# Expert stage of a two-block transformer kernel: the down product from native fp32 to three split passes

## The chip, the cores and the metric

The kernel runs on one core of a Trainium2 chip as a single program. The metric is the device time of one execution in microseconds (us); lower is better. Three executions of the kernel before took 2968.38, 2960.40 and 2960.74 us, median 2960.74 us.

## What is computed

The reference is a first block (a modulated token mixer and a mixture-of-experts feed-forward layer over 512 tokens of width 1024) and a second block (two attention layers, each with a convolutional feed-forward layer). The change concerns the mixture of experts. Each token goes to 8 of 64 experts, and for every block of at most 128 rows that belong to one expert the reference does:

```python
xb = hpad[rows]
y = (jax.nn.silu(xb @ we_gate[e]) * (xb @ we_up[e])) @ we_down[e]
acc = acc.at[rows].add(y * rw[:, None].astype(y.dtype))
```

`we_gate[e]` and `we_up[e]` are 1024x256, `we_down[e]` is 256x1024, all fp32.

## The kernel before, in words

The program is a row of stages, each a block in which every engine runs its own instructions in order and engines meet through semaphores. `experts` is the longest stage. It handles 66 blocks: 62 written out, one expert each, and the rest in a loop whose length is found at run time.

The work of one block b is spread over the engines:

- **SyncE** (SP queue) loads the expert's weights as three transfers of 1 MB, two of gate and up weights (`load_gu`) and one of down weights (`load_dn`), into `raw` buffers of which every one exists twice. The order of issue is gate-and-up of block b, then down of block b-2. Line 1297 issues all of them.
- **ScalarE** (ACT) writes the high part of each quarter of the gate-and-up weights, rounded to the fp32r type (`high_gu`, L1395), the high part of the turned rows (`high_x`, L1405), SiLU (L1400), and copies PSUM to SBUF: the block's result (`copy_y`, L1413) and the turned activations (`copy_act`, L1418).
- **VectorE** (DVE) writes the low parts, the number less its high part (`low_gu`, L1446; `low_x`, L1453), multiplies gate and up (`activate`, L1459), reads the token numbers of a later block from PSUM (L1469, L1474), aims its store (L1464), and prepares the selection of a block after that (`choose`, L1489).
- **GpSimd** (POOL) issues the indirect gather of rows of block b+2 (L1524) and the indirect store of block b-2 (L1531).
- **TensorE** (PE) runs, in step b: `find(b+2)`, a small product (L1333); `gate_and_up(b)`, 8 pieces of the depth in three passes each (L1351); `turn(b+1)`, 8 transposes (L1340); `down(b-1)` (L1363); and `turn_act(b)`, 2 transposes (L1371).

A product in three passes takes high by high, high by low and low by high, with fp32r operands. `down` alone takes its operands unsplit: the turned activations `act_t` in fp32 and the raw down weights:

```python
for k in range(2):
    mm = pe.matmul(ps[:, BY + n, :], at[:, k * P:(k + 1) * P], ex.chunk(GU + k, s)[:, half],
                   start=(k == 0), stop=(k == 1))
```

The order on each engine is fixed by the function `step` of that engine. On ScalarE step b is: three `high_gu` of b, `silu(b-1)`, `high_x(b)`, the fourth `high_gu` of b, `copy_y(b-2)`, `copy_act(b-1)`. On VectorE it is: three `low_gu` of b, `activate(b-1)`, `low_x(b)`, the fourth `low_gu` of b, `aim(b-2)`, `read_tokens(b+2)`, `choose(b+3)`. On GpSimd it is: `gather(b+2)`, `store(b-2)`.

The attention stages, later in the program, split their weights in the same way, with the high parts on ScalarE and the low parts on GpSimd (L2096).

Of the kernel before, what the change touches and what calls it, by code (L numbers as in the profile page):

```python
# [1241 lines left out]
def experts(m, d, scratch, ex):  # L1242
# [9 lines left out]
    with stack:  # L1252
# [7 lines left out]
        at = sb("act_t", [P, 2 * P])  # L1260
# [3 lines left out]
         a_done, a_turned, at_done, y_made, y_out, target_done, own_s, issued, pool_seen) = (  # L1264
            sem(n) for n in ("picked", "listed_at", "listed", "xt_turned", "xt_high", "xt_low", "gu_high", "gu_low",
                             "gu_used", "sg_done", "a_done", "a_turned", "at_done", "y_made",
# [26 lines left out]
        with nc.Block() as block:  # L1293
            @block.sync
            def _(sp):
# [8 lines left out]
                def load_dn(b, s, e):  # L1304
                    sp.wait_ge(y_made, value(2 * b - 2))
                    load(GU // 2, s, e)
# [19 lines left out]
            def _(pe):  # L1326
# [28 lines left out]
                def down(c, s, h):  # L1355
                    pe.wait_ge(at_done, value(c + 1))
                    pe.wait_ge(ex.arrived(GU + 1, s), value(16 * h + 16))
                    for n in range(2):
                        if some(2 * c + (n - 2)):
                            pe.wait_ge(y_out, value(2 * c + (n - 1)))  # L1360
                        half = slice(n * 512, (n + 1) * 512)
                        for k in range(2):
                            mm = pe.matmul(ps[:, BY + n, :], at[:, k * P:(k + 1) * P], ex.chunk(GU + k, s)[:, half],  # L1363
                                           start=(k == 0), stop=(k == 1))
                        mm.then_inc(y_made, 1)
# [24 lines left out]
            def _(act):  # L1390
# [23 lines left out]

                def copy_act(b):
                    act.wait_ge(a_turned, value(b + 1))
                    act.wait_ge(y_made, value(2 * b))
                    act.activation(at[:], ps[:, BA, 0:2 * P], ACT.Copy).then_inc(at_done, 1)  # L1418

                def step(b, s, h):  # L1420
# [8 lines left out]
                    if some(b - 1):  # L1429
                        copy_act(b - 1)  # L1430

# [5 lines left out]
                copy_act(end - 1)  # L1437
                copy_y(end - 1, 1, half - 1)

            @block.vector  # L1440
            def _(dve):
# [14 lines left out]
                def activate(b):  # L1456
                    dve.wait_ge(sg_done, value(b + 1))
                    dve.wait_ge(a_turned, value(b))
                    dve.scalar_tensor_tensor(a[:], ps[:, BG, D_EXP:], row(found, b, 2), sg[:], ALU.mult, ALU.mult).then_inc(a_done, 1)  # L1459

# [30 lines left out]
                def step(b, s, h):  # L1491
# [8 lines left out]
                    read_tokens(b + 2, s, h + 1)  # L1500
                    choose(b + 3)
# [11 lines left out]
                activate(end - 1)  # L1513
                aim(end - 2, 0, half - 1)
# [3 lines left out]
            def _(pool):  # L1518
# [14 lines left out]

                def step(b, s, h):
                    gather(b + 2, s)
                    if some(b - 2):
# [6 lines left out]
                end, half = Count(pairs, 2, FIRST), Count(pairs, 1, FIRST // 2)  # L1543
                store(end - 2, 0, half - 1)
# [912 lines left out]
```

## Time and profile before

| | |
|---|---|
| median of 3 runs | 2960.74 us |
| the profiled execution | 2961.6 us |
| its span | 2959.8 us |
| granted TensorE clock, mean | 0.927 |
| PE busy | 2577.0 us (87%) |
| DVE busy | 1650.0 us (56%) |
| ACT busy | 1165.8 us (39%) |
| POOL busy | 253.6 us (9%) |
| expert stage, first to last gate-and-up product | 664.2 to 1334.2 us |

The span is the time from the first to the last instruction. Shares are over the whole program; the stage in question has shares of its own. A busy PE is modelled from the starts of its instructions, so neighbouring matmuls overlap in the rows: their spacing is read from their starts.

### The profile page before, as it was taken

Reading aid. Unit: us, or ns where it says so; the run is one execution under the profiler, and the core shown is the slowest. Engines: PE = TensorE matmul, PEld = TensorE weight load, DVE = VectorE, ACT = ScalarE, POOL = GpSimd, SP = SyncE. Lnnn points to the kernel's source line nnn. Section 1 sums busy time; section 2 is a strip of 40 time slices with the busy share of each in tenths; the row PEclk is TensorE's granted clock in tenths of the full one; section 3 lists DMA queues with packets and bytes.
Section 4 is the critical chain, followed back from the end, with each engine's and each line's share of the span. In section 5 each row is a group of like instructions: output and inputs, shape, how many; then the busy total and the mean of one; then the engine's idle time right before and its main releaser. Section 6 shows DMA issues by size and latency. Waiting matters only on the chain. (4 is left out here: it accounts for less than half of the span.)

```text
span 2959.8 us, 30515 instructions
## 1 busy us (share of the span) xinstructions
PE 2577.0 (87%) x10494; PEld 1794.2 (61%) x10494; DVE 1650.0 (56%) x2733; ACT 1165.8 (39%) x1797; POOL 253.6 (9%) x186
## 2 busy tenths in 40 slices
PE   6998998469999999992599988999968884899998
PEld 2443556337776777671366666888746662678886
DVE  2392663437777777776355545636535546366473
ACT  2003432216666666661233334424323323354242
POOL 0000000001111222120122100000012210000000
PEclk9999898589999999996699999999989996899999
DMA  6102121318999999986211013232221101222322
GB/s 275 57 0 83 63 86 57 144 38 322 360 350 357 358 358 348 365 325 244 85 64 43 0 57 112 83 113 90 71 107 43 43 0 43 71 85 92 107 84 73
DMA packets 77263, 418.70 MB, mean 141 GB/s; under 512 B 17312, under 2 KB 17440, under 8 KB 40160
## 3 DMA queue, kind: packets, MB, share of 16 engines
q1 hardware_dynamic: 57856, 383.67, 35.1%
q0 software_dynamic: 19296, 33.60, 3.1%
q8 instruction: 63, 1.03, 0.1%
q14 instruction: 48, 0.39, 0.0%
HBM read 415.10 MB, written 38.80 MB: 153 GB/s over the span
## 5 line engine op out<-in xcount | busy, mean ns | idle before, releaser
L1446 DVE TENSOR_TENSOR w_gu_low<-raw,w_gu_high 128x1024 fp32r<-128x1024 f32 x264 | 322.8, 1223 | 121.7 <-ACT w_gu_high L1395 108.9
L1395 ACT ACTIVATE w_gu_high<-raw 128x1024 fp32r<-128x1024 f32 x264 | 279.8, 1061 | 109.0 <-PE banks L1351 107.8
L2270 PE MATMUL banks<-h_high,w_high 128*128 128x512 f32 x704 | 276.8, 393 | 33.0 <-DVE w_low L2333 33.0
L2270 PE MATMUL banks<-h_low,w_high 128*128 128x512 f32 x704 | 275.6, 391 | 0.0
L2270 PE MATMUL banks<-h_high,w_low 128*128 128x512 f32 x704 | 275.4, 391 | 0.0
L1363 PE MATMUL banks<-raw,act_t 128*128 128x512 f32 x528 | 237.6, 593 | 0.9 <-ACT act_t L1418 0.9
L1351 PE MATMUL banks<-w_gu_high,x_t_high 128*128 128x512 f32 x528 | 213.9, 405 | 2.0 <-DVE x_t_low L1453 2.0
L1351 PE MATMUL banks<-w_gu_high,x_t_low 128*128 128x512 f32 x528 | 207.9, 394 | 0.0
L1351 PE MATMUL banks<-w_gu_low,x_t_high 128*128 128x512 f32 x528 | 207.6, 393 | 0.0
L2333 DVE TENSOR_TENSOR w_low<-raw,w_high 128x2048 fp32r<-128x2048 f32 (+2 forms) x76 | 152.9, 2012 | 87.3 <-ACT w_high L2298 87.2
L2298 ACT ACTIVATE w_high<-raw 128x2048 fp32r<-128x2048 f32 (+2 forms) x76 | 128.0, 1684 | 170.8 <-PE banks L2280 152.7
L2270 PEld LDWEIGHTS banks<-h_high,w_high 128*128 128x128 f32 x704 | 133.3, 189 | 65.6 <-issue 38.0
L1524 POOL DMA_INDIRECT x_rows<-h_rows,token_i x68 | 69.7, 1024 | 1172.8 <-DVE token_i L1474 1164.3
L1363 PEld LDWEIGHTS banks<-raw,act_t 128*128 128x128 f32 x528 | 95.2, 190 | 95.8 <-issue 94.7
L2270 PEld LDWEIGHTS banks<-h_high,w_low 128*128 128x128 f32 x704 | 133.1, 189 | 27.9
L2270 PEld LDWEIGHTS banks<-h_low,w_high 128*128 128x128 f32 x704 | 133.2, 189 | 27.5
L2280 PE MATMUL banks<-hidden_high,w_high 128*128 128x512 f32 x352 | 141.6, 402 | 2.5 <-DVE w_low L2333 2.5
L2310 ACT ACTIVATE conv<-up,vec 128x512 f32<-128x512 f32 x88 | 70.6, 815 | 184.9 <-DVE up L2348 184.9
L2280 PE MATMUL banks<-hidden_high,w_low 128*128 128x512 f32 x352 | 137.1, 390 | 0.0
L2280 PE MATMUL banks<-hidden_low,w_high 128*128 128x512 f32 x352 | 137.0, 389 | 0.0
L1351 PEld LDWEIGHTS banks<-w_gu_high,x_t_low 128*128 128x128 f32 x528 | 99.7, 189 | 22.7
L590 PE MATMUL banks<-h,w_in 128*128 128x512 f32 (+3 forms) x256 | 101.9, 561 | 12.9 <-DMA w_in<-in_w_in 12.9
(356 smaller groups left out, 4865.9 us busy)
## 6 DMA issues: line engine op xcount, KB each, us to landing
raw<-in_w_e SPq DMA_DIRECT2D x198, 1024.0 KB, 9.1
raw<-in_w_up SPq DMA_DIRECT2D x44, 1024.0 KB, 4.8
w_ada<-in_w_ada_later SPq DMA_DIRECT2D x16, 1024.0 KB, 4.8
expert_rows<-y_rows SPq DMA_DIRECT2D x16, 1024.0 KB, 11.3
w_qkv<-in_w_even SPq DMA_DIRECT2D x8, 1536.0 KB, 6.3
raw<-in_w_down SPq DMA_DIRECT2D x16, 768.0 KB, 4.2
w_qkv<-in_w_odd SPq DMA_DIRECT2D x8, 1536.0 KB, 6.3
raw<-in_w_down SPq DMA_DIRECT2D x16, 640.0 KB, 3.9
```

Of the source, the lines that this page charges most:

```text
L590: mm = pe.matmul(bank[0:cols, 0:t[1]], wt(name)[:, k, j * P:j * P + cols], m.h[:, k, t[0]:t[0] + t[1]], start=(k == 0), stop=(k == KT - 1))
L1351: mm = pe.matmul(ps[:, BG, :], xp[:, k, :], wp[:, j, :], start=(k == 0 and i == 0), stop=(k == KT - 1 and i == 2))
L1363: mm = pe.matmul(ps[:, BY + n, :], at[:, k * P:(k + 1) * P], ex.chunk(GU + k, s)[:, half], start=(k == 0), stop=(k == 1))
L1395: act.activation(w_gu[c].high[:].rearrange("p j n -> p (j n)"), ex.chunk(c, s), ACT.Copy).then_inc(gu_high, 1)
L1446: dve.tensor_tensor(w_gu[c].low[:].rearrange("p j n -> p (j n)"), ex.chunk(c, s), w_gu[c].high[:].rearrange("p j n -> p (j n)").bitcast(F3 ...
L1524: pool.indirect_dma_start(xg[s][:], None, scratch["h_rows"], bass.IndirectOffsetOnAxis(ap=token_i[s][:, 0:1], axis=0), bounds_check=SEQ - ...
L2270: mm = pe.matmul(ps[:, 2 * s + c, :], wp[:, at:at + P], hp[:, k, :], start=(k == 0 and i == 0), stop=(k == KT - 1 and i == 2))
L2280: mm = pe.matmul(ps[:, 4 + s, :], wp[:, k * P:(k + 1) * P], hp[:, k, :], start=(k == 0 and i == 0), stop=(k == b - a - 1 and i == 2))
L2298: act.activation(w[s].high[:, 0:cols], raw[s][:, 0:cols], ACT.Copy).then_inc(high_done, 1)
L2310: act.activation(y[s][:, c, :], up[s][:, c, :], ACT.Identity, scale=tap(t, c, 2), bias=tap(t, c, 3)).then_inc(tap0, 1)
L2333: dve.tensor_tensor(w[s].low[:, 0:cols], raw[s][:, 0:cols], w[s].high[:, 0:cols].bitcast(F32), ALU.subtract).then_inc(low_done, 1)
```

## The change

The down product takes the same three passes as gate and up. The activations get a high part, written by ScalarE in `copy_act`, and a low part, written by VectorE in a new `low_act`. The down weights get a high part, written by ScalarE in a new `high_dn` as four instructions of 128x512, and a low part, written by GpSimd in a new `low_dn`, also four. There is one buffer `w_dn` for each part. The raw buffer of the down weights is free for its next load once `low_dn` has read it, and no longer once the product is made.

```diff
-        at = sb("act_t", [P, 2 * P])
+        at, w_dn = Split(sb, "act_t", [P, 2 * P]), Split(sb, "w_dn", [P, 2, D])
...
                 def load_dn(b, s, e):
-                    sp.wait_ge(y_made, value(2 * b - 2))
+                    sp.wait_ge(dn_low, value(4 * b - 4))
...
                 def down(c, s, h):
                     pe.wait_ge(at_done, value(c + 1))
-                    pe.wait_ge(ex.arrived(GU + 1, s), value(16 * h + 16))
...
                         for k in range(2):
-                            mm = pe.matmul(ps[:, BY + n, :], at[:, k * P:(k + 1) * P], ex.chunk(GU + k, s)[:, half],
-                                           start=(k == 0), stop=(k == 1))
+                            pe.wait_ge(dn_low, value(4 * c + (2 * n + k + 1)))
+                            for i, (ap, wp) in enumerate(at.passes(w_dn)):
+                                mm = pe.matmul(ps[:, BY + n, :], ap[:, k * P:(k + 1) * P], wp[:, k, half],
+                                               start=(k == 0 and i == 0), stop=(k == 1 and i == 2))
                         mm.then_inc(y_made, 1)
...
+                def high_dn(c, s, h):
+                    act.wait_ge(ex.arrived(GU, s), value(16 * h + 16))
+                    for n in range(2):
+                        if some(2 * c + (n - 2)):
+                            act.wait_ge(y_made, value(2 * c + (n - 1)))
+                        for k in range(2):
+                            act.activation(w_dn.high[:, k, n * 512:(n + 1) * 512], ex.chunk(GU + k, s)[:, n * 512:(n + 1) * 512],
+                                           ACT.Copy).then_inc(dn_high, 1)
...
-                    act.activation(at[:], ps[:, BA, 0:2 * P], ACT.Copy).then_inc(at_done, 1)
+                    act.activation(at.high[:], ps[:, BA, 0:2 * P], ACT.Copy).then_inc(at_high, 1)
...
                     if some(b - 1):
                         copy_act(b - 1)
+                        high_dn(b - 1, *later(s, h, -1))
...
+                def low_act(b):
+                    dve.wait_ge(at_high, value(b + 1))
+                    dve.tensor_tensor(at.low[:], ps[:, BA, 0:2 * P], at.high[:].bitcast(F32), ALU.subtract).then_inc(at_done, 1)
...
                     read_tokens(b + 2, s, h + 1)
+                    if some(b - 1):
+                        low_act(b - 1)
                     choose(b + 3)
...
+                def low_dn(c, s):
+                    for n in range(2):
+                        for k in range(2):
+                            half = slice(n * 512, (n + 1) * 512)
+                            pool.wait_ge(dn_high, value(4 * c + (2 * n + k + 1)))
+                            pool.tensor_tensor(w_dn.low[:, k, half], ex.chunk(GU + k, s)[:, half],
+                                               w_dn.high[:, k, half].bitcast(F32), ALU.subtract).then_inc(dn_low, 1)
...
                 def step(b, s, h):
                     gather(b + 2, s)
+                    if some(b - 1):
+                        low_dn(b - 1, (s + 1) % 2)
                     if some(b - 2):
                         store(b - 2, *later(s, h, -2))
```

The order of ScalarE's instructions over one step in the middle of the expert stage, in the changed kernel (`raw_0_11` and `raw_1_11` are the two copies of the raw buffers; line numbers are the changed kernel's):

```order
L1414 ACTIVATE y_block_15<-banks 128x512 x2
L1428 ACTIVATE act_t_high<-banks 128x256
L1422 ACTIVATE w_dn_high<-raw_0_11 128x512 x4
L1396 ACTIVATE w_gu_high<-raw_0_11 128x1024 x3
L1401 ACTIVATE silu_gate<-banks 128x256
L1406 ACTIVATE x_t_high<-banks 128x512 x2
L1396 ACTIVATE w_gu_high<-raw_0_11 128x1024
```

The four new copies stand between the copy of the activations and the first three quarters of the next block's gate-and-up weights. Nothing else has changed its place.

The order on GpSimd over one step, before:

```order
L1524 DMA x_rows_15<-h_rows,token_i_15 128x1024
L1531 DMA y_rows<-y_block_15,target_i_15 4096x1024
```

and in the changed kernel:

```order
L1543 DMA x_rows_15<-h_rows,token_i_15 128x1024
L1558 TENSOR_TENSOR w_dn_low<-raw_0_11,w_dn_high 128x512 x4
L1550 DMA y_rows<-y_block_15,target_i_15 4096x1024
```

The four subtractions stand behind a gather and ahead of a store.

## Rows read from the trace of the kernel before

**Rows 1.** One stretch of the expert stage: columns are us, busy us of each engine (instructions), granted PE clock, DMA share, GB/s

```profile
1000.00:1100.00 100.00, 100.00 (x451) 70.48 (x450) 71.62 (x108) 68.64 (x97) 21.04 (x20) 1.00 0.98 359
```

**Rows 2.** Timeline of TensorE over one block: start, us, operation

```profile
1002.32 0.48 PE L1351 MATMUL banks<-w_gu_high,x_t_high 128*128 128x512 f32 x1
...
1007.22 0.39 PE L1351 MATMUL banks<-w_gu_high,x_t_high 128*128 128x512 f32 x1
1007.45 0.39 PE L1351 MATMUL banks<-w_gu_low,x_t_high 128*128 128x512 f32 x1
...
1008.78 3.60 PE L1363 MATMUL banks<-raw,act_t 128*128 128x512 f32 x8
1012.22 0.38 PE L1371 MATMUL banks<-const,act 128*128 128x128 f32 x2
...
1012.54 0.48 PE L1351 MATMUL banks<-w_gu_high,x_t_high 128*128 128x512 f32 x1
```

**Rows 3.** Timeline of DVE, ACT and POOL in that block, with idle time before

```profile
1002.69 0.38 ACT L1418 ACTIVATE act_t<-banks 128x256 f32<-128x256 f32 x1
...
1003.73 1.02 POOL L1524 DMA_INDIRECT x_rows<-h_rows,token_i  x1 [7.91 <-DVE token_i L1474]
...
1004.05 1.06 ACT L1395 ACTIVATE w_gu_high<-raw 128x1024 fp32r<-128x1024 f32 x1 [0.97 <-PE banks L1351]
...
1005.05 1.00 POOL L1531 DMA_INDIRECT y_rows<-y_block,target_i  x1 [0.31 <-issue]
1005.14 1.23 DVE L1446 TENSOR_TENSOR w_gu_low<-raw,w_gu_high 128x1024 fp32r<-128x1024 f32 x1 [1.68 <-ACT w_gu_high L1395]
...
1007.89 1.23 DVE L1446 TENSOR_TENSOR w_gu_low<-raw,w_gu_high 128x1024 fp32r<-128x1024 f32 x1
...
1008.55 1.08 ACT L1405 ACTIVATE x_t_high<-banks 128x512 fp32r<-128x512 f32 x2
...
1010.62 1.22 DVE L1446 TENSOR_TENSOR w_gu_low<-raw,w_gu_high 128x1024 fp32r<-128x1024 f32 x1
```

**Rows 4.** DVE's groups by line from 1000 to 1300 us: busy, mean ns, idle before

```profile
L1446 DVE TENSOR_TENSOR w_gu_low<-raw,w_gu_high 128x1024 fp32r<-128x1024 f32 x117 | 143.1, 1223 | 53.7 <-ACT w_gu_high L1395 48.5
L1453 DVE TENSOR_TENSOR x_t_low<-banks,x_t_high 128x512 fp32r<-128x512 f32 x59 | 37.8, 681 | 0.0
L1489 DVE TENSOR_TENSOR pick<-const,dest 128x512 bf16<-128x512 f32 x26 | 17.7, 682 | 0.0
L1459 DVE SCALAR_TENSOR_TENSOR act<-banks,found,silu_gate 128x256 f32<-128x256 f32 x29 | 13.9, 478 | 0.0
```

**Rows 5.** One line of ScalarE in the attention stages: min/median/max ns

```profile
L1745 ACT ACTIVATE h_high<-o x16: 612/613/629, 1715.2 to 2506.0; 128x512 fp32r<-128x512 f32 x16
```

**Rows 6.** Timeline of POOL and DVE at the start of the first attention stage

```profile
1444.79 2.35 POOL L2096 TENSOR_TENSOR w_v_low<-w_qkv,w_v_high 128x1024 fp32r<-128x1024 f32 x1
...
1446.42 1.88 DVE L2081 TENSOR_TENSOR rope<-rope,rstd 128x512 f32<-128x512 f32 x2 [14.47 <-DMA amask<-in_amask]
...
1451.44 2.79 DVE L2016 TENSOR_TENSOR crossed<-banks,rope 32x512 f32<-32x512 f32 x4
1451.85 2.34 POOL L2096 TENSOR_TENSOR w_q_low<-w_qkv,w_q_high 128x1024 fp32r<-128x1024 f32 x1 [4.71 <-ACT w_q_high L1979]
```

**Rows 7.** Those two lines of DVE in both attention stages: min/median/max ns

```profile
L2081 DVE TENSOR_TENSOR rope<-rope,rstd x4: 678/964/1276, 1446.4 to 2182.6; 128x512 f32<-128x512 f32 x4
...
L2016 DVE TENSOR_TENSOR crossed<-banks,rope x128: 679/686/695, 1451.4 to 2429.1; 32x512 f32<-32x512 f32 x128
```

**Rows 8.** DMA from 1000 to 1100 us: totals

```profile
DMA packets 6994, 35.87 MB, mean 359 GB/s; under 512 B 2072, under 2 KB 2072, under 8 KB 3169
```

**Rows 9.** A stretch in which the input projection's weights are loaded, columns as rows 1

```profile
60.00:74.00 14.00, 9.31 (x17) 4.13 (x18) 0.45 (x1) 0.22 (x1) 0.00 (x0) 0.69 0.98 414
```

**Rows 10.** SP's issue of down weights at 1012.41 us, and its time to landing

```profile
1012.41 0.33 SPq L1297 DMA_DIRECT2D raw<-in_w_e  x1
...
raw<-in_w_e SPq DMA_DIRECT2D x1, 1024.0 KB, 13.2
```

More of the change, by code:

```diff
@@ L1263, in experts @@
         (picked, listed_at, listed, xt_turned, xt_high, xt_low, gu_high, gu_low, gu_used, sg_done,
-         a_done, a_turned, at_done, y_made, y_out, target_done, own_s, issued, pool_seen) = (
+         a_done, a_turned, at_high, at_done, dn_high, dn_low, y_made, y_out, target_done, own_s, issued, pool_seen) = (
             sem(n) for n in ("picked", "listed_at", "listed", "xt_turned", "xt_high", "xt_low", "gu_high", "gu_low",
-                             "gu_used", "sg_done", "a_done", "a_turned", "at_done", "y_made",
+                             "gu_used", "sg_done", "a_done", "a_turned", "at_high", "at_done", "dn_high", "dn_low", "y_made",
                              "y_out", "target_done", "own", "issued", "pool_seen"))
@@ L1437, in _ @@
                 copy_act(end - 1)
+                high_dn(end - 1, 1, half - 1)
                 copy_y(end - 1, 1, half - 1)
@@ L1513, in _ @@
                 activate(end - 1)
+                low_act(end - 1)
                 aim(end - 2, 0, half - 1)
@@ L1543, in _ @@
                 end, half = Count(pairs, 2, FIRST), Count(pairs, 1, FIRST // 2)
+                low_dn(end - 1, 1)
                 store(end - 2, 0, half - 1)
```

## The prediction

> **What bounds the kernel now.** I read the stretches of the expert stage first, then the timeline of one block, then the groups by line. In the stretches PE is busy for 100.00 of 100 us at a granted clock of 1.00, while DVE and ACT are busy for 71.62 and 68.64 us and POOL for 21.04 [rows 1]. In the timeline one block's first gate-and-up pass starts at 1002.32 and the next one's at 1012.54 [rows 2], so a block takes 10.22 us, and nothing stands idle on PE between. So the stage is bound by PE's own work, but the next limits are near: the DMA engines have a share of 0.98 [rows 1].
>
> **What the change removes.** The down product is eight PE instructions that start at 1008.78 and are followed by the next operation at 1012.22 [rows 2]: 3.44 us, 0.43 each. Passes with fp32r operands of the same 128x512 shape start 0.23 us apart [rows 2]. The change makes twelve of them, 12 x 0.228 = 2.74 us. PE is relieved of 0.70 us a block, and PE alone would need 9.52 us. Over 66 blocks that would be 46 us.
>
> **What it adds, engine by engine.**
>
> ACT: four copies SBUF to SBUF of 128x512. The same form takes 613 ns [rows 5]. Back to back a copy starts about 0.1 us before the one ahead has ended: the two of x_t_high take 1.08 us together [rows 3], where the pair would be 1.19 apart from that. So the four cost 4 x 0.52 = 2.1 us. ACT's load goes from 0.6864 x 10.22 = 7.0 us to 9.1 us, which still fits into 9.52 with hardly a gap.
>
> DVE: `low_act`, 128x256 with one input in PSUM. Nearest is activate, 478 ns for 128x256 [rows 4]; I take 0.45. DVE's load goes from 7.3 to 7.8 us.
>
> POOL: four subtractions of 128x512. The trace has them at twice the size, 2.35 us [rows 6]. Half of that, 1.17 us, is the lower bound, 1.3 with some fixed part the upper. I take 1.17, since the row is almost all slope if DVE's pair (1223 for 1024, 682 for 512 elements [rows 4]) is a guide: its fixed part is 0.14 us. That is 4.7 us a block, and POOL goes from 2.1 to 6.8. Taken alone it fits.
>
> SP: `load_dn` waits for `low_dn` instead of for the product. `low_dn` of a block is done before its product, so this wait is over sooner, and the loads ahead of it in the queue still set the time of issue: nothing gained or lost.
>
> **The price that decides: two engines at one port.** Loads add up only if the engines don't hinder each other, and the attention stages show that they do. A POOL subtraction runs from 1444.79 to 1447.14. DVE starts the first of two multiplications with both inputs in SBUF at 1446.42 [rows 6]. The shortest of its line takes 678 ns; the longest took 1276 [rows 7], and since the pair takes 1.88 us [rows 6] this one is it: it ended at 1447.70, 0.55 us after POOL, so it did all but its first 0.13 us once POOL was through. But `crossed`, with one input in PSUM, takes 2.79 us for four beside a POOL subtraction [rows 6], and 679 to 695 ns in all 128 cases [rows 7]. So a DVE operation whose inputs both lie in SBUF stands still while a POOL subtraction runs. This agrees with the Trainium skill (SBUF — State Buffer, Who interferes with whom): such a DVE instruction contends with a GpSimd instruction that reads SBUF, and the second to be issued blocks fully. No row here shows POOL as the second.
>
> In the expert stage five of DVE's operations a block are of that kind: four of w_gu_low (1223 ns) and one of pick (682) [rows 4]. Those of x_t_low and activate read PSUM and are free.
>
> I lay one block out, from the start of its gate-and-up product (1002.32 is zero). ACT ends the copy of act_t at 0.75 [rows 3], the four new copies at 2.9, and the first three w_gu_high at 3.9, 4.9 and 5.9; the first ended at 2.8 before [rows 3]. POOL's gather starts at 1.4 and with its 0.3 us behind is over at 2.7 [rows 3]. Then POOL and DVE take turns:
>
> - POOL's first subtraction 2.7 to 3.9; first w_gu_low 3.9 to 5.1
> - second subtraction 5.0 to 6.2; second w_gu_low 6.1 to 7.3
> - third subtraction 7.2 to 8.4; third w_gu_low 8.3 to 9.5
> - fourth subtraction 9.4 to 10.6, beside activate and x_t_low, which end at 11.1; fourth w_gu_low 11.1 to 12.3
>
> The third w_gu_low ended at 6.8 before [rows 3]. The next gate-and-up product needs x_t_low at 11.1. The down product needs the fourth subtraction at 10.6, then 0.7 us for its last three passes and 0.3 for what follows: 11.6. So a block takes 11.1 to 11.6 us; the fourth w_gu_low now ends after the next product has begun, where it used to end 0.7 us ahead, which moves the gather and with it POOL. DVE's own sum says the same: 7.8 of work and three POOL operations in front of its w_gu_low, 3 x 1.05 = 3.15, is 10.9, and some of its old idle 1.68 us ahead of the first w_gu_low [rows 3] stays. I take 11.4.
>
> **The sum.** 64 blocks x (11.40 - 10.22) = +75.5 us. At the end the last block's weights are split with nothing beside: 0.6 + 4 x 1.17 + 0.7 = 6.0 us in place of 3.44, +2.5. The profiled execution took 2961.6 us; with +78 it would be 3039.6. That execution was 0.9 us above the median, so 3039. For 10.9 to 11.9 us a block the same sum gives 3006 to 3070, the forecast's own range. PE then idles about 1.9 us a block in short pieces; I price no loss of clock for this, since the granted clock was 1.00 in the stretch.
>
> **Rivals.**
>
> *No exclusion here, and the DMA sets the pace: faster.* The turning point is plain: if a POOL subtraction holds DVE for so little that DVE's waits stay under 10.2 - 7.8 = 2.4 us a block in all, and they don't lie on the way to x_t_low, the block gets shorter. It can't reach 9.52. A block moves 3.67 MB (35.87 MB in 100 us [rows 8]). At the rate of this stage brought to full share, 359 / 0.98 = 366 GB/s, that needs 10.0 us. Loads alone went faster elsewhere, 414 GB/s at 0.98 [rows 9], so with luck it is 9.52, PE's own. At 10.0 the gain is 0.22 x 64 = 14, less 2.5 at the end: 2949; at 9.52, 2918. For it: PE is the only bound today. Against it: [rows 6, 7]. Chance 0.17, of which 0.05 for under 2942.
>
> *No change.* The exclusion is weak, and the down weights come late. They must be there when ACT has copied act_t, 0.75 us into the next block, and no longer only at the down product. Those issued at 1012.41 took 13.2 us, to 1025.6 [rows 10], while ACT would want them at 1022.76 + 0.75 = 1023.5. ACT would stand 2 us with the next w_gu_high behind it, in those blocks in which the DMA queue is long. Then 10.2 us a block remain: 2961. The Trainium skill (DMA: Bandwidth & Descriptors, Specifications) gives about 358 GB/s as what HBM delivers to one core; by that 3.67 MB need 10.25 us, and no change could be faster than today. The 414 GB/s of [rows 9] are above that figure, so the measurement decides and I leave the faster case its chance. Chance 0.07.
>
> *The exclusion is partial.* POOL and DVE interleave within an instruction: 10.3 to 10.9 us a block, 2970 to 3006. Chance 0.15.
>
> *The exclusion is worse.* POOL never waits and also stops a DVE operation in flight, so that DVE bears all four: 7.8 + 4.7 = 12.5 us, +146 + 2.5 = 3109. Chance 0.08.
>
> The forecast itself has 0.53. That the passes aren't what they seem is no rival: the gate-and-up product has the same form.
>
> **How the numbers follow.** Runs of this kernel tell a change from none at about 0.3%, 9 us. Faster 0.17, same 0.07, slower 0.15 + 0.53 + 0.08 = 0.76. The range goes from 2942, which takes in the DMA-bound case with 0.1 us a block to spare, to 3095, which leaves most of the worst case out; outside are 0.05 below and 0.08 above.
>
> **What would show it.** In the changed profile: in the stretches of the stage PE at 80 to 88 of 100 us, no DMA wait, DMA share at 0.85 to 0.90. In DVE's groups w_gu_low at 1.9 to 2.1 us mean against 1223 ns, x_t_low still at 681. POOL's w_dn_low at 1.17 to 1.3 us undisturbed and up to 2.3 where DVE was first. PE waiting for w_dn_low and x_t_low. The forecast is wrong if w_gu_low keeps 1223 ns, or if PE's idle time ends on a transfer, or on ACT.

## Result and profile after

The changed kernel takes 3172.2 us (median of 4 runs, 3170.3 to 3173.6), the kernel before 2962.5 in the same measurement. The ratio is 1.0703, with a 95% interval of 1.0687 to 1.0719: slower by 7%, and 133 us above the forecast.

The same stretch of the stage as [rows 1], now from the changed kernel (us, busy us of PE, PE weight load, DVE, ACT and POOL, granted PE clock, DMA share, GB/s):

```profile
1000.00:1100.00 100.00, 85.15 (x377) 67.29 (x377) 91.90 (x86) 67.72 (x104) 61.36 (x47) 0.88 0.76 281
```

PE, which was busy all the time, is at 85 of 100 us. DVE has gone from 71.6 to 91.9 us although a block gives it only one more short operation. The DMA share has fallen from 0.98 to 0.76: the transfers now wait for the kernel, and no engine's wait for one shows in the stage from 1000 to 1300 us. A block (from one first gate-and-up pass to the next) takes 13.41 us on average in place of 10.23; over 64 blocks that is 204 of the 210 us.

The groups of the page for the two subtractions, over the whole span, and DVE's by duration (min/median/max ns):

```profile
L1458 DVE TENSOR_TENSOR w_gu_low<-raw,w_gu_high 128x1024 fp32r<-128x1024 f32 x264 | 608.6, 2343 | 75.0 <-ACT w_gu_high L1396 75.0
L1558 POOL TENSOR_TENSOR w_dn_low<-raw,w_dn_high 128x512 fp32r<-128x512 f32 x264 | 334.5, 1295 | 5.8 <-ACT w_dn_high L1422 4.3
```

```profile
L1458 DVE TENSOR_TENSOR w_gu_low<-raw,w_gu_high x264: 1205/1211/6685, 658.2 to 1533.3; 128x1024 fp32r<-128x1024 f32 x132
L1558 POOL TENSOR_TENSOR w_dn_low<-raw,w_dn_high x264: 1261/1297/1318, 678.3 to 1551.0; 128x512 fp32r<-128x512 f32 x132
```

w_gu_low's mean has gone from 1223 ns [rows 4] to 2343. But its median is 1211: three of four are as fast as ever, and in 63 of the 66 blocks one takes 5.3 to 6.7 us. POOL's subtraction never takes more than 1318 ns, so POOL never waits for DVE. The timeline of one block (start, us, operation, [idle before]), POOL first, then DVE:

```profile
1012.21 1.02 POOL L1543 DMA_INDIRECT x_rows<-h_rows,token_i  x1 [5.31 <-DVE token_i L1490]
1013.26 5.06 POOL L1558 TENSOR_TENSOR w_dn_low<-raw,w_dn_high 128x512 fp32r<-128x512 f32 x4
1018.49 1.81 POOL L1550 DMA_INDIRECT y_rows<-y_block,target_i  x1 [0.17 <-issue]
1025.60 1.02 POOL L1543 DMA_INDIRECT x_rows<-h_rows,token_i  x1 [5.30 <-DVE token_i L1490]
```

```profile
1013.46 5.94 DVE L1458 TENSOR_TENSOR w_gu_low<-raw,w_gu_high 128x1024 fp32r<-128x1024 f32 x1 [1.20 <-ACT w_gu_high L1396]
```

```profile
1013.46 8.21 DVE L1458 TENSOR_TENSOR w_gu_low<-raw,w_gu_high 128x1024 fp32r<-128x1024 f32 x3 [1.20 <-ACT w_gu_high L1396]
1021.60 0.47 DVE L1471 SCALAR_TENSOR_TENSOR act<-banks,found,silu_gate 128x256 f32<-128x256 f32 x1
1021.99 1.27 DVE L1465 TENSOR_TENSOR x_t_low<-banks,x_t_high 128x512 fp32r<-128x512 f32 x2
1023.19 1.21 DVE L1458 TENSOR_TENSOR w_gu_low<-raw,w_gu_high 128x1024 fp32r<-128x1024 f32 x1
...
1024.57 0.15 DVE L1490 TENSOR_SCALAR token_i<-found 128x1 int32<-128x1 f32 x1
```

The first w_gu_low stands for all four of POOL's subtractions, which end at 1018.32, and ends 1.08 us after them: nearly its whole 1.21 us was still to do. From there the rows close a ring from gather to gather: 1.05 us to the first subtraction, 5.06 for the row of four, 1.08 for the held w_gu_low, 2.27 for the next two, 1.59 for act and x_t_low, 1.13 for the fourth w_gu_low, 0.33 to the end of token_i, and 0.88 until POOL starts the next gather: 13.39 us. Every link is on POOL or DVE, and none on PE. PE only waits at the side, for act and x_t_low (1000 to 1300 us: us in total, times, longest):

```profile
PEld banks L1372 <- DVE act L1471: 40.5, 22, 3.2
...
PE banks L1351 <- DVE x_t_low L1465: 13.8, 22, 0.7
```

### The profile page after: what moved, and what is told of

Read it like the earlier page. It is cut to its first block and busy times, and to the rows that moved or that the text cites. A ratio compares the mean times of both kernels' runs of the same rounds, so it can differ in the third digit from the quotient of the medians.

```text
span 3171.8 us, 31796 instructions
## 1 busy us (share of the span) xinstructions
PE 2648.6 (84%) x10758; PEld 1907.3 (60%) x10758; DVE 1956.6 (62%) x2799; ACT 1302.0 (41%) x2061; POOL 634.1 (20%) x450
## 5 line engine op out<-in xcount | busy, mean ns | idle before, releaser
L1458 DVE TENSOR_TENSOR w_gu_low<-raw,w_gu_high 128x1024 fp32r<-128x1024 f32 x264 | 608.6, 2343 | 75.0 <-ACT w_gu_high L1396 75.0
L1558 POOL TENSOR_TENSOR w_dn_low<-raw,w_dn_high 128x512 fp32r<-128x512 f32 x264 | 334.5, 1295 | 5.8 <-ACT w_dn_high L1422 4.3
L1351 PE MATMUL banks<-w_gu_high,x_t_high 128*128 128x512 f32 x528 | 252.1, 477 | 41.7 <-DVE x_t_low L1465 41.6
L1351 PE MATMUL banks<-w_gu_low,x_t_high 128*128 128x512 f32 x528 | 241.4, 457 | 0.0
L1351 PE MATMUL banks<-w_gu_high,x_t_low 128*128 128x512 f32 x528 | 239.9, 454 | 0.0
L2126 POOL TENSOR_TENSOR w_q_low<-w_qkv,w_q_high 128x1024 fp32r<-128x1024 f32 x16 | 37.9, 2369 | 738.5 <-ACT w_q_high L2009 738.5
L1351 PEld LDWEIGHTS banks<-w_gu_high,x_t_high 128*128 128x128 f32 x528 | 121.6, 230 | 75.0 <-DVE x_t_low L1465 45.2
L1422 ACT ACTIVATE w_dn_high<-raw 128x512 fp32r<-128x512 f32 x264 | 143.9, 621 | 0.0
L1351 PEld LDWEIGHTS banks<-w_gu_high,x_t_low 128*128 128x128 f32 x528 | 120.1, 227 | 30.5
L1351 PEld LDWEIGHTS banks<-w_gu_low,x_t_high 128*128 128x128 f32 x528 | 121.6, 230 | 26.7
```

Source lines behind the costliest of these rows:

```text
L1351: mm = pe.matmul(ps[:, BG, :], xp[:, k, :], wp[:, j, :], start=(k == 0 and i == 0), stop=(k == KT - 1 and i == 2))
L1422: act.activation(w_dn.high[:, k, n * 512:(n + 1) * 512], ex.chunk(GU + k, s)[:, n * 512:(n + 1) * 512], ACT.Copy).then_inc(dn_high, 1)
L1458: dve.tensor_tensor(w_gu[c].low[:].rearrange("p j n -> p (j n)"), ex.chunk(c, s), w_gu[c].high[:].rearrange("p j n -> p (j n)").bitcast(F3 ...
L1558: pool.tensor_tensor(w_dn.low[:, k, half], ex.chunk(GU + k, s)[:, half], w_dn.high[:, k, half].bitcast(F32), ALU.subtract).then_inc(dn_low, 1)
L2126: pool.tensor_tensor(ws[part].low[:], w[s][:, part], ws[part].high[:].bitcast(F32), ALU.subtract).then_inc(low_done, 1)
```

## Experiments

The cuts show the lines that matter; the semaphore counts that keep buffers, loads and the last block in order are left out.

**1. Is it POOL's subtractions at all, and how do they add up?** The kernel before gets subtractions on POOL behind the gather, from two buffers that nobody else uses; nothing waits for them. PE's passes, ACT's copies and the loads stay as they were.

```
 gather(b + 2, s)
+for i in range(4):          # idle_two_subtractions: range(2)
+    pool.tensor_tensor(idle_out[i][:], idle_in[0][:], idle_in[1][:], ALU.subtract)
```

> The kernel before, and in each block of the expert stage GpSimd does four subtractions of 128x512 from two tiles of its own that nobody reads, behind its gather. Nothing waits for them. Theory A (a subtraction on GpSimd holds every VectorE operation with two SBUF inputs, and a row of them holds it to the end of the row): w_gu_low of the first quarter rises from 1.22 to about 6 us, the block from 10.22 to 12.4 to 13.1 us, the time from 2961 to 3100 to 3150 us. Theory B (the loss of the change lies in ScalarE's four copies, the late down weights and the order of waits): GpSimd has time to spare, so 10.22 us a block and 2961 us. Theory C (turns, as the prediction had it): w_gu_low at about 2.3 us for three of four, 11.3 us a block, 3030 us.

Measured: 3155.9 us, ratio 1.0646 (1.0624 to 1.0667). 13.34 us a block in all but a few, and 61 w_gu_low of 5.3 to 6.6 us: theory A, though block and time lie just above the ranges I gave it. So the subtractions alone, without a consumer, make nearly the whole loss, and the changed kernel's three passes give nothing back.

> The kernel before with two idle POOL subtractions of 128x512 a block behind the gather in place of four; nothing waits for them. Theory (a POOL subtraction stops every DVE operation with both inputs in SBUF for its whole length, even one that is under way, and only what exceeds DVE's slack lengthens the block): four cost 13.34 - 10.23 = 3.1 us a block for a row of 5.1 us, so 2.0 us of it lay in slack; two make a row of 2.57 us, of which 0.5 to 0.7 us is too much: 10.7 to 10.9 us a block, 2994 to 3007 us. One w_gu_low a block at 3.5 to 4 us, the others 1.21. If the loss were in proportion to the number of subtractions (each costs 0.78 us a block whatever the slack), 11.8 us a block and 3060 us. If POOL has to be under way for long before DVE is stopped, 10.23 us and 2963.

Measured: 3002.9 us, ratio 1.0137 (1.0110 to 1.0165), 10.88 us a block in nearly all, as expected. The ring with a row of 2.56 in place of 5.06 us is 13.39 - 2.50 = 10.89. Above PE's 10.22 every subtraction costs its full length; the loss in proportion to their number (11.8 us) is refuted.

This kernel also shows who holds whom, and that my "even one that is under way" was wrong. Two blocks of it, POOL and then DVE:

```profile
823.81 1.03 POOL L1526 DMA_INDIRECT x_rows<-h_rows,token_i  x1 [5.63 <-issue]
824.86 3.79 POOL L1541 TENSOR_TENSOR idle_out<-idle_in 128x512 fp32r<-128x512 f32 x2
...
833.66 1.01 POOL L1526 DMA_INDIRECT x_rows<-h_rows,token_i  x1 [3.04 <-DVE token_i L1476]
834.68 2.56 POOL L1541 TENSOR_TENSOR idle_out<-idle_in 128x512 fp32r<-128x512 f32 x2
```

```profile
824.05 1.22 DVE L1448 TENSOR_TENSOR w_gu_low<-raw,w_gu_high 128x1024 fp32r<-128x1024 f32 x1 [0.84 <-ACT w_gu_high L1397]
825.43 4.30 DVE L1448 TENSOR_TENSOR w_gu_low<-raw,w_gu_high 128x1024 fp32r<-128x1024 f32 x2 [0.15 <-ACT w_gu_high L1397]
...
834.26 6.35 DVE L1448 TENSOR_TENSOR w_gu_low<-raw,w_gu_high 128x1024 fp32r<-128x1024 f32 x3 [0.88 <-ACT w_gu_high L1397]
```

In the first block w_gu_low starts at 824.05, 0.81 us ahead of POOL's first subtraction, and takes its plain 1.22; POOL's two then take 3.79 in place of 2.56, and DVE's next two 4.30: turns, as forecast. In the second, w_gu_low starts at 834.26, only 0.42 ahead of 834.68, and POOL's two take 2.56 while the three w_gu_low take 6.35. I took all such pairs in six kernels (this one, idle_four_subtractions, the changed one, and filler_on_pe, memset_ahead_of_row and memsets_inside_row below): DVE operations with both inputs in SBUF that started before POOL's first subtraction of a row and would still run at its start. The 206 that started 0.66 us or less ahead stood until the row was over, in all six kernels. The 11 that started 0.77 us or more ahead were free; these come from three of the kernels only (this one, idle_four_subtractions, memset_ahead_of_row). None lies between.

**2. Reading or only being busy?** The same four instructions as memsets and as copies.

> The kernel before with four memsets of 128x512 on GpSimd in each block in place of the four subtractions of the first experiment: GpSimd writes SBUF and reads none. Theory A in its narrow form (it is the reading that holds VectorE): 10.22 us a block, 2961 us, w_gu_low at 1.22 us. Theory A in a wide form (any GpSimd work on SBUF holds VectorE): w_gu_low lengthened by the length of the memsets, 2980 us or more. Theory B: 2961 us.

Measured: 2963.4 us, ratio 1.0001 (0.9991 to 1.0012).

```profile
L1448 DVE TENSOR_TENSOR w_gu_low<-raw,w_gu_high x264: 1210/1225/1228, 656.4 to 1325.9; 128x1024 fp32r<-128x1024 f32 x132
```

No w_gu_low is touched by an instruction that only writes, though 129 of the 264 run beside a memset.

> The kernel before with four idle POOL copies of 128x512 a block, SBUF to SBUF, that is with one input read in place of two. Theory (any POOL instruction that reads SBUF holds DVE): one w_gu_low a block is longer by about the row's length; at 0.7 to 1.1 us a copy the row is 2.8 to 4.4 us, of which 2.0 lie in slack, so 11.0 to 12.6 us a block and 3012 to 3115 us. Rival (only a POOL operation with two inputs holds DVE): w_gu_low at 1223 ns in all cases, 10.23 us a block, 2963 us, as with the memsets.

Measured: 2964.6 us, ratio 1.0011 (0.9998 to 1.0023): no change that can be told. But this isn't the rival, for the hold is there (groups from 1000 to 1100 us):

```profile
L1448 DVE TENSOR_TENSOR w_gu_low<-raw,w_gu_high 128x1024 fp32r<-128x1024 f32 x40 | 62.3, 1588 | 13.7 <-ACT w_gu_high L1397 13.4
L1542 POOL COPY idle_out<-idle_in 128x512 f32<-128x512 f32 x40 | 38.4, 1000 | 0.0
```

One input read is enough to hold DVE: 4 x (1588 - 1223) = 1.5 us a block. Alone, the row of copies is short (2.3 us), and that hold still fits into DVE's slack. I had expected copies of 0.7 to 1.1 us; alone they take 0.61, and the time I gave, 3012 us or more, was too high for that. The order decides here too, at a smaller lead: the 18 w_gu_low that started 0.27 us or less ahead of a row were held (2.87 us or more for their 1.22), and 15 of the 16 that started 0.28 us or more ahead were nearly free, with the copies then taking 1.5 us in turns. This agrees with the Trainium skill (SBUF — State Buffer, Who interferes with whom): a DVE instruction with two SBUF inputs contends with a GpSimd instruction that reads SBUF, not with one that only writes it.

**3. What are the other parts of the change worth?** First the low parts of the down weights are left out, so that POOL has nothing to do (the low buffer holds zeros); then DVE computes them, in two instructions of 128x1024, and ACT copies in the same size.

```
-                            pe.wait_ge(dn_low, value(4 * c + (2 * n + k + 1)))
+                            pe.wait_ge(dn_high, value(4 * c + (2 * n + k + 1)))
...
-                    if some(b - 1):
-                        low_dn(b - 1, (s + 1) % 2)       # POOL
```

> The changed kernel without GpSimd's low parts of the down weights: the low tile is zero, set once, so the product leaves out the pass high by low in effect but still makes it. ScalarE's copies, the twelve passes, low_act and the early wait for the down weights stay; the product waits for the high parts. Theory A: the block falls from 13.4 us to what PE (9.52) or the DMA (10.0) allow, w_gu_low back at 1.22 us, 2918 to 2965 us. Theory B: it stays above 12 us, over 3080 us.

Measured: 2977.0 us, ratio 1.0044 (1.0027 to 1.0061), 10.39 us a block on average: far from theory B, but 12 us above the range of theory A.

> The changed kernel with the low parts of the down weights on VectorE as two instructions of 128x1024 at the end of its step, and the high parts as two of 128x1024; GpSimd only gathers and stores. Theory A: VectorE has 7.3 + 0.4 + 2.3 = 10.0 us of work a block and nothing holds it, so 10.1 to 10.6 us a block, 2955 to 2990 us. Theory B: ScalarE's load and the order of waits are the same as in the change, so it stays above 12 us, over 3080 us.

```
-                    if some(b - 1):
-                        low_dn(b - 1, (s + 1) % 2)       # POOL
+                    if some(b - 1):
+                        low_dn(b - 1, (s + 1) % 2)       # DVE, behind choose(b + 3)
```

Measured: 2984.8 us, ratio 1.0073 (1.0056 to 1.0090), 10.45 us a block, inside theory A's range. Off POOL, then, 187 of the 210 us are gone. What remains in both is above all one wait (1000 to 1300 us, the version without low parts and the version on DVE):

```profile
ACT w_dn_high L1423 <- DMA raw<-in_w_e: 56.1, 29, 3.0
```

```profile
ACT w_dn_high L1421 <- DMA raw<-in_w_e: 52.9, 28, 3.1
```

Once a block ACT stands for the down weights, with the next w_gu_high behind it. That is the forecast's "the down weights come late", up to 3.1 us a time. That this wait makes the 10.4 us is tested in experiment 7.

**4. The clock.** PE's granted clock had fallen from 1.00 to 0.88. Two matmuls a block into a bank that nobody reads fill part of PE's waits.

```
 def turn_act(b):
+    pe.matmul(ps[:, 7, :], ident, CONST.of(m.const, "mask_fwd", 0, 512), start=True, stop=True)
     pe.wait_ge(a_done, value(b + 1))
...
 find(b + 2)
+pe.matmul(ps[:, 7, 0:256], ident, CONST.of(m.const, "mask_fwd", 0, 256), start=True, stop=True)
 gate_and_up(b)
```

> The changed kernel with two more PE matmuls a block into a bank that nobody reads: a 128x512 one ahead of the wait for act, a 128x256 one ahead of the gate-and-up product. They fill PE's waits and change no other engine's work. It tells how much of the loss is the clock (granted 0.88 in the stage). Theory A (the held w_gu_low makes nearly all of it, the clock 0.3 to 1 us a block): the granted clock goes to 0.97 or more and the block from 13.41 to 12.6 to 13.1 us: 3118 to 3152 us. Rival (the clock is the larger part of the 2 us that the hold's count leaves): 11.5 to 12.3 us, 3050 to 3100 us. If the clock stays at 0.88 the fillers only cost: up to 0.65 us a block, 3172 to 3215 us, and the question stays open.

Measured: 3173.0 us, ratio 1.0707 (1.0690 to 1.0724), exactly as the changed kernel.

```profile
1000.00:1100.00 100.00, 91.53 (x414) 69.10 (x413) 91.07 (x88) 69.56 (x107) 60.46 (x47) 0.94 0.76 280
```

Half the lost clock is back, and the block still takes 13.41 us. None of the three cases I gave came out as written: the clock rose to 0.94 and not to 0.97, and the time stands at the lower end of the third, which was for a clock that stays at 0.88. At first I had taken the lower clock for a part of the loss; the ring above has no PE work in it, and the time doesn't follow the clock. The lower clock goes with PE's waits and is not a cause of the time.

**5. Why are there no turns?** Four runs ask what lets DVE in. In the first POOL's row waits for the step's first w_gu_low.

```
 def low_dn(c, s):
+    pool.wait_ge(gu_low, value(4 * c + 9))
```

> The changed kernel, but POOL's four subtractions wait until DVE has done the first w_gu_low of the step, so that another w_gu_low is under way when the first subtraction comes. Theory (who is at the port first keeps it: in the runs so far a DVE operation that started up to 0.25 us after the gather's start kept its 1.22 us and the first subtraction then took 1.57, while one that started 0.39 us or more after it stood until the whole row of subtractions was through; so the order decides between turns and a held row): w_gu_low at 1.2 to 2.3 us and none at 5 or more; the subtractions partly at 2.2 us; w_gu_low two and three lose nothing or one subtraction, the fourth is behind the rest of the row. 11.2 to 11.7 us a block: 3028 to 3062 us, about what the forecast said for turns. Rival (a row of POOL's subtractions always passes whole, whoever came first): one w_gu_low a block at 5 us or more, and with the later start 13.4 to 14.5 us a block: 3172 us and above.

Measured: 3226.8 us, ratio 1.0878 (1.0853 to 1.0903).

```profile
L1458 DVE TENSOR_TENSOR w_gu_low<-raw,w_gu_high x264: 1215/1961/2355, 662.6 to 1582.0; 128x1024 fp32r<-128x1024 f32 x132
```

Half right: no w_gu_low is above 2.36 us, so turns come where DVE is ahead. The time is the rival's, for another reason: the row starts later and is longer, the down product waits for its end, and behind the product ACT has the y_block copy, act_t_high, four w_dn_high and only then the w_gu_high that the first w_gu_low needs: 13.1 to 15.1 us a block. After a semaphore wait a subtraction has no such place ahead either: w_gu_low that started 0.17 to 0.27 us before it were free here.

> The changed kernel with one POOL memset of 128x512 (0.54 us, it did not hold DVE in idle_four_memsets) between the gather and the four subtractions. Theory (a subtraction queued behind the gather takes the port about 0.3 us after the gather's start, before it is seen to start; behind a memset it does so only about the start of the memset): w_gu_low, which starts 0.54 to 1.22 us after the gather, now comes first; turns as in vector_goes_first, 11.2 to 11.8 us a block, 3028 to 3070 us. Rival (the row holds DVE however it is queued, from the gather on): only 0.54 us are added to the row, 13.4 to 14.0 us a block, 3172 to 3210 us, with w_gu_low at 6 us or more once a block.

Measured: 3193.0 us, ratio 1.0769 (1.0747 to 1.0792). The memset pushed the row back by 0.5 us, and that was too little:

```profile
1023.35 0.54 POOL L1558 MEMSET idle_out<- 128x512 f32 x1
1023.84 5.07 POOL L1563 TENSOR_TENSOR w_dn_low<-raw,w_dn_high 128x512 fp32r<-128x512 f32 x4
```

```profile
1023.43 8.83 DVE L1459 TENSOR_TENSOR w_gu_low<-raw,w_gu_high 128x1024 fp32r<-128x1024 f32 x3 [1.04 <-ACT w_gu_high L1397]
```

DVE starts 0.41 us ahead of the row and is held. In five blocks it started 0.93 us or more ahead, and was free; those periods are 12.12 us. The bound between 0.66 and 0.77 us holds here too, measured from the subtraction and not from the gather.

> The changed kernel with a POOL memset of 128x512 ahead of the second, third and fourth subtraction, none ahead of the first. Theory (back to back, the next subtraction is queued before DVE's waiting operation gets the port; behind a memset it isn't): the first w_gu_low is held by one subtraction alone, about 2.5 to 3.2 us in place of 5.3 to 6.6, and then turns: 11.3 to 12.2 us a block, 3035 to 3095 us. Rival (DVE stands until POOL has no subtraction left): the row grows to 5.1 + 1.6 = 6.7 us and w_gu_low with it to 7 or 8 us: 15.0 us a block, 3275 us.

Measured: 3252.7 us, ratio 1.0969 (1.0948 to 1.0989), 14.78 us in nearly all blocks: the rival. A gap of about 0.5 us in POOL's row does not let DVE in; w_gu_low is held for the memsets as well, though a memset alone holds nobody:

```profile
1035.56 8.00 DVE L1459 TENSOR_TENSOR w_gu_low<-raw,w_gu_high 128x1024 fp32r<-128x1024 f32 x1 [0.51 <-ACT w_gu_high L1397]
```

Three rows at the very end, in the loop that handles the last blocks, are the exception: there w_gu_low took 1.3 to 2.3 us, the later subtractions 1.8, and the block 12.5 us, with the same gap. Why is open; it may be that the next subtraction is queued later there.

If a subtraction that is queued behind other work has its place about 0.7 us before it is seen to start, a gap of 0.5 us is covered and one of 1.0 us is not. That gives the deciding run:

```
 pool.wait_ge(dn_high, value(4 * c + (2 * n + k + 1)))
+if 2 * n + k:
+    for i in range(2):
+        pool.memset(idle_out[2 * (2 * n + k - 1) + i][:], 1.0)
 pool.tensor_tensor(w_dn.low[:, k, half], ...)
```

> The changed kernel with two POOL memsets (0.52 us each, 1.04 together) ahead of the second, third and fourth subtraction. Theory (a subtraction queued on POOL behind other POOL work has its place at the port 0.66 to 0.77 us before it is seen to start, so that a gap of 0.52 us, as in memsets_inside_row, never lets DVE in, and one of 1.04 does): the first w_gu_low is held by one subtraction alone, 2.4 to 3.2 us, none is above 4, subtractions take up to 2.3 us where a w_gu_low is ahead of them, and the block takes 11.5 to 12.8 us though POOL's row has grown: 3045 to 3130 us. Rival (DVE stands until POOL has no subtraction left, whatever lies between): the row is 5.1 + 3.1 = 8.2 us, w_gu_low 8.3 to 9.8 us once a block, 16.4 us a block, 3365 us.

Measured: 3098.1 us, ratio 1.0462 (1.0437 to 1.0488), 11.9 us in most blocks. With more work on POOL the kernel is 74 us faster than the changed one.

```profile
L1459 DVE TENSOR_TENSOR w_gu_low<-raw,w_gu_high x264: 1205/1323/2994, 657.4 to 1457.5; 128x1024 fp32r<-128x1024 f32 x132
```

```profile
1025.88 5.80 DVE L1459 TENSOR_TENSOR w_gu_low<-raw,w_gu_high 128x1024 fp32r<-128x1024 f32 x3 [2.00 <-ACT w_gu_high L1397]
```

```profile
1024.79 1.30 POOL L1565 TENSOR_TENSOR w_dn_low<-raw,w_dn_high 128x512 fp32r<-128x512 f32 x1
1026.04 0.98 POOL L1563 MEMSET idle_out<- 128x512 f32 x2
1026.99 1.37 POOL L1565 TENSOR_TENSOR w_dn_low<-raw,w_dn_high 128x512 fp32r<-128x512 f32 x1
```

In the gap DVE's first operation runs (1025.88 to 1027.18), and the next two take 2.3 us each: held by one subtraction, not by the row. One part of the expectation missed: no subtraction took 2.3 us; the longest is 1.49.

**6. Do turns cost what the forecast said?** POOL's second to fourth subtraction wait for the step's first to third w_gu_low; the row begins early.

```
 pool.wait_ge(dn_high, value(4 * c + (2 * n + k + 1)))
+if 2 * n + k:
+    pool.wait_ge(gu_low, value(4 * c + (8 + 2 * n + k)))
```

> The changed kernel, in which POOL's second, third and fourth subtraction wait until DVE has done the first, second and third w_gu_low of the step; the first subtraction waits as before for nothing more. It makes the turns that the forecast assumed, with the row begun early. Theory (the order at the port decides, and turns cost what the forecast's timetable said): w_gu_low never above 3.9 us (two subtractions), 11.2 to 12.2 us a block, 3028 to 3090 us. Rival (turns are no cheaper than the held row, since the down product then waits for the last subtraction and ACT's copies behind it): 13.4 to 14.5 us a block as in vector_goes_first, 3172 to 3240 us, with PE waiting for w_dn_low.

Measured: 3093.3 us, ratio 1.0442 (1.0415 to 1.0470), 12.07 us in most blocks; no w_gu_low above 2.57 us. The time is just above the range I gave, the block inside it. Turns are 79 us cheaper than the held row, and still 130 us dearer than the kernel before. The ring now goes through PE: the row takes 8.17 us (1019.53 to 1027.70), then the last passes of the down product and find, up to the start of found, take 1.36, and found, token_i and the gather 2.54: 12.07.

```profile
1019.53 1.31 POOL L1561 TENSOR_TENSOR w_dn_low<-raw,w_dn_high 128x512 fp32r<-128x512 f32 x1
1022.09 5.62 POOL L1561 TENSOR_TENSOR w_dn_low<-raw,w_dn_high 128x512 fp32r<-128x512 f32 x3 [1.25 <-DVE w_gu_low L1458]
...
1030.29 1.28 POOL L1544 DMA_INDIRECT x_rows<-h_rows,token_i  x1 [0.62 <-issue]
```

```profile
1029.06 0.17 DVE L1485 TENSOR_REDUCE found<-banks 128x3 f32<-128x9 f32 x1 [0.21 <-PE banks L1333]
```

**7. A version that beats both.** The low parts on DVE, and SP issues a block's down weights ahead of the gate-and-up weights that came before them.

```
-                        load_gu(b, s, owners[2 + s])
                         load_dn(b - 2, s, owners[s])
+                        load_gu(b, s, owners[2 + s])
```

> The low parts of the down weights on DVE (as in low_parts_on_vector, 10.45 us a block), and SP issues the down weights of a block ahead of the gate-and-up weights that it now issues before them. Theory (late down weights are what holds ACT's w_dn_high, 3.1 us where it waits): the wait goes and the block comes to 9.6 to 10.05 us, DVE's own load being about 9.8: 2925 to 2952 us. Rival (the DMA engines' rate sets the pace, whichever load is first): the wait moves to w_gu_high, and 10.2 to 10.5 us a block stay: 2961 to 2985 us. A third: SP now waits for the down buffer ahead of the gate-and-up loads, these come late, 10.6 or more: over 2990 us.

Measured: 2948.8 us, ratio 0.9959 (0.9945 to 0.9973): faster than before by 0.4%, than the change by 7%. The columns are those of the row at the start of the section on the result:

```profile
700.00:800.00 100.00, 100.00 (x523) 82.93 (x521) 99.66 (x146) 89.05 (x126) 40.77 (x21) 1.00 1.00 376
1000.00:1100.00 100.00, 98.36 (x508) 81.33 (x507) 98.16 (x142) 86.16 (x123) 40.17 (x22) 1.00 0.97 367
```

Up to about 950 us a block takes 9.66 us, with PE and DVE both full. After that most take 10.0 to 11.0, the DMA engines give 361 to 369 GB/s in place of 376, and ACT waits for w_gu_high's raw weights (41.6 us in 300). Why the rate falls is open; no run asks it.

> As change_without_low_parts (the down product in three passes with ACT's high parts, the low parts left out, so that nobody computes them), and SP issues a block's down weights ahead of the gate-and-up weights. It shows what the three passes are worth once neither POOL nor late down weights are in the way. Theory (PE alone needs 9.52 us): 9.52 to 9.8 us a block, 2915 to 2936 us. Rival (the DMA rate of 359 to 367 GB/s sets it, 10.0 us for 3.67 MB): 9.9 to 10.1 us, 2940 to 2955 us.

Measured: 2944.2 us, ratio 0.9931 (0.9907 to 0.9954). 9.56 us a block up to about 900 us, then mostly 9.8 to 10.9, and 9.95 on average: over the whole stage the rival's numbers, at its start the theory's. So the three passes alone give what the forecast said of PE, 9.52, while the weights come; DVE's extra work costs 0.1 us a block on top early in the stage and nothing that shows in the average. The control, the old kernel with the new order of loads:

> The kernel before, with the down weights of a block issued ahead of the gate-and-up weights that it issues before them; no split of the down product. Theory (PE's own 10.22 us a block bound the kernel, and the order of the loads is worth nothing without the three passes): 10.22 us a block, 2961 us. Rival (the order of the loads is itself a gain): 2945 to 2955 us. A third: SP waits for the down product ahead of the gate-and-up loads, these come late, 2975 us or more.

Measured: 2968.0 us, ratio 1.0015 (1.0004 to 1.0026): no gain by the order alone, if anything a loss of 4 us. The 0.4% are the three passes', once DVE makes the low parts and the down weights come in time.

## Why the prediction was wrong

- **What bounds the kernel before, and what PE gains:** right. The passes cost what was said, and the block comes to 9.56 us where POOL and late weights are out of the way.
- **ACT and DVE:** right. Four copies take 2.19 us (2.1 said), act_t_low 0.415 (0.45 said).
- **POOL's subtraction:** 1.295 us, not 1.17. It has a fixed part after all; the upper bound of 1.3 was the better choice. Back to back the four take 5.06 us in place of 4.7, so 0.4 us a block.
- **A POOL instruction that reads SBUF holds DVE's operations with two SBUF inputs:** right, and shown by the memsets against the copies and subtractions.
- **The step that failed: "Then POOL and DVE take turns."** The timetable let DVE in between POOL's subtractions; it did not ask whether the next subtraction is ahead of DVE's waiting operation. The first w_gu_low instead stands for the whole row, 5.06 us, and the gaps of experiment 5 fit a next subtraction that has its place before the last one has ended. Where turns were made to come (turns_by_waits) a block took 12.07 us and the kernel 3093 us; the timetable had 11.1 to 11.6, its upper end from the down product, and 11.4 was taken. So of the 133 us missed, about 79 lie in the turns that did not come and 54 in the timetable's sizes, as far as this run, in which POOL also stands 1.25 us ahead of its second subtraction, can stand for free turns.
- **The timetable didn't close either.** It starts the gather at 1.4 us into the block, but its fourth w_gu_low ends at 12.3. With the ring's 0.33 and 0.88 us behind that, the next gather would start at 13.5, which is 12.1 us after the first. The prediction says that the gather moves, and took 11.4 all the same. Measured with turns: 12.07, although the path there goes through PE.
- **The rival that came true** was "the exclusion is worse", with 0.08 of the chance. Its mechanism, POOL never waits and DVE bears all four, is what the rows show. Its price, 12.5 us and 3109 us, was too low: it added up DVE's work (7.8) and POOL's (4.7) and left out that POOL's row starts only when DVE has made token_i and the gather is over. In the ring of the rows DVE's links are 6.40 us (1.08 + 2.27 + 1.59 + 1.13 + 0.33; the rest of its 7.8 lies beside the gather), POOL's row 5.06, and the gather with the wait ahead of it 1.93 (0.88 + 1.05): 13.39. That a DVE operation "in flight" is stopped was only apparent, since POOL's subtraction had its place first: where it hadn't, DVE's operation ran through.
- **Late down weights:** the mechanism is real (the DMA waits of experiment 3) and was hidden here, because the slower block leaves the loads time. It is worth 0.4 to 0.5 us a block as soon as POOL is out of the way (10.39 and 10.45 us against 9.95 on average with the early load), and it turned a gain into a loss there.
- **The DMA bound:** the forecast said 10.0 us at 366 GB/s, 9.52 with luck. Each of the two runs with the early load has both: 9.56 or 9.66 us a block early in the stage, mostly 10 to 11 late.
- **Clock:** priced at nothing, and that was right for the time (filler_on_pe), though the granted clock fell to 0.88.
- **Of the signs that it named**, PE at 80 to 88 of 100 us (85.15), x_t_low at its old length (674 ns) and PE's wait for x_t_low came. w_gu_low's mean is 2343 ns and not 1.9 to 2.1 us, the DMA share 0.76 and not 0.85 to 0.90, no subtraction took 2.3 us, and PE waited for w_dn_low once in 300 us, for 0.2.

## What to carry to other kernels

Don't move work to GpSimd because its column is empty: if it reads SBUF, and VectorE has operations with both inputs in SBUF, add the whole row of back-to-back GpSimd subtractions to VectorE's path, not one of them. Before summing an engine's load, follow the ring of who starts whom; here GpSimd's row began with a gather that needed VectorE's last small operation, so POOL's row and most of VectorE's work ran in series. And when weights get a new consumer that wants them earlier, move their load too.

## What the runs showed of the hardware

- A GpSimd subtraction of 128x512 that follows other GpSimd work blocks a VectorE operation with two SBUF inputs that starts up to 0.66 us before the subtraction is seen to start, and not one that starts 0.77 us or more before it. The first holds in six kernels (206 cases), the second in three (11 cases). Behind a semaphore wait that has only just ended there is no such lead: in vector_goes_first the 39 that started 0.17 to 0.27 us ahead were free. The Trainium skill (Perfetto Trace Analysis, GPSIMD Engine Instruction) says that the start shown for such an instruction is its first read, after it has gone to the execution queue and its program has begun. This would explain a place taken ahead of the start; the runs show the 0.7 us, not what happens in them.
- Four subtractions in a row hold VectorE for all of them (5.3 to 6.7 us for a 1.21 us operation); one memset of 0.52 us between them did not help except in three rows of the last blocks, two did.
- Copies with one input behave otherwise. In 44 of 66 rows three of 0.6 us pass, and the fourth lets VectorE in and takes 1.6. In 15 more, with w_gu_low 0.28 us or more ahead, the two take turns from the first copy on. Why a row of copies breaks and one of subtractions doesn't is open.
- How long a GpSimd indirect DMA takes depends on what VectorE had begun before it. In the kernel before, 57 of 66 stores take 1.0 us although a w_gu_low starts 0.09 us into them, and the six that start while one is under way take 1.5 to 2.0. In the changed kernel 62 of 66 start with a w_gu_low under way, and take 1.8 us. The w_gu_low beside them keep their 1.21 us.
